# One-core transformer stack: the first norm by channel halves, lambdas later, shift's modulation sums among the first projections, FFN step 0 in other banks, two square roots folded into one

## The reference, cut to what matters

```python
# block 1, two layers l = 0, 1
mod = silu(c) @ ada_w[l] + ada_b[l]        # 1024 -> 6 * 1024
shift1, scale1, gate1, shift2, scale2, gate2 = split(mod, 6)
h = rms_norm(x, norm1_g[l]) * (1 + scale1) + shift1
z = h @ w_in[l]                            # q, k, v, ga, gb, gates
lam = exp(sum(lambda_q1 * lambda_k1)) - exp(sum(lambda_q2 * lambda_k2)) + lambda_init
u = causal_depthwise_conv(ga * sigmoid(gb), 31 taps)
x = x + (1 + gate1) * ((g_attn * y_attn + g_conv * y_conv) @ w_out[l])
h2 = rms_norm(x, norm2_g[l]) * (1 + scale2) + shift2
x = x + (1 + gate2) * ((silu(h2 @ Wg) * (h2 @ Wu)) @ w_ffn_out[l])
# end of block 1, and of block 2: a norm of the stream, and at once the norm of the next block
x = rms_norm(x, final_g); h = rms_norm(x, next_g)
```

## Time and profile before

| what | value |
|---|---|
| median of 3 runs | 2552.34 us (2552.05 to 2553.14) |
| the profiled execution | 2553.99 us, its span 2552.1 us |
| PE busy | 2396.1 us, 94% |
| DVE busy | 1965.9 us, 77% |
| ACT busy | 1442.5 us, 57% |
| PE clock, mean of the span | 0.972 of full |
| read from HBM | 649.32 MB, 255 GB/s |

### The profile page before, as it was taken

How to read it: one execution, slowest core, us unless ns; L and a number is a source line. 1 busy time by engine, 2 the same in 40 slices (tenths; PEclk the granted TensorE clock), 3 DMA queues, 4 the chain that set the end, 5 groups by cost and what they waited for, 6 DMA issues and landing times.

```text
span 2552.1 us, 32705 instructions
## 1 busy us (share of the span) xinstructions
PE 2396.1 (94%) x11965; PEld 2001.3 (78%) x11965; DVE 1965.9 (77%) x1889; ACT 1442.5 (57%) x1418; POOL 17.6 (1%) x33
## 2 busy tenths in 40 slices
PE   4996999998999899799999969999999999999997
PEld 4865788867788798797887968888888888888886
DVE  6888778687687656675445748898989888888897
ACT  2553433546443454464434527777777777777775
POOL 0000000000000000000000000000000000000000
PEclk8997999999999899899999979999999999999998
DMA  8358699534598445455555429999999999999995
GB/s 326 124 173 297 226 317 321 187 121 164 167 329 300 145 163 187 131 170 173 188 183 165 165 83 331 361 340 350 350 340 359 333 366 334 366 334 366 331 368 180
DMA packets 435139, 651.79 MB, mean 255 GB/s; under 512 B 20688, under 2 KB 324432, under 8 KB 435040
## 3 DMA queue, kind: packets, MB, share of 16 engines
q1 hardware_dynamic: 432880, 643.59, 74.0%
q0 software_dynamic: 2160, 6.85, 0.8%
HBM read 649.32 MB, written 1.05 MB: 255 GB/s over the span
## 4 chain that ended last, share of the span: by engine, by line
PE 84%; DVE 9%; ACT 3%; issue 3%; DMA 1%; SPq 0%; DVEq 0%; POOL 0%; ACTq 0%
PE pair L1894 25%; PE pair L1896 25%; PE pair L1895 25%; DVE rest L1079 2%; PE pair L1929 2%; PE tb L2107 2%; DVE aw L1417 1%; ACT head L677 1%; DVE aw L1098 1%; PE pair L2017 1%; PE tb L1972 1%; DMA x<-in_x 1%; ACT aw L706 1%; DVE hT L1200 0%; DVE gat L1825 0%
## 5 line engine op out<-in xcount | busy, mean ns | idle before, releaser
L1079 DVE TENSOR_TENSOR rest<-raw,head 128x2048 fp32r<-128x2048 f32 x546 | 1249.2, 2292 | 296.2 <-ACT head L677 276.4
L677 ACT ACTIVATE head<-raw 128x2048 fp32r<-128x2048 f32 x546 | 1043.2, 1912 | 308.4 <-PE pair L1896 284.9
L1894 PE MATMUL pair<-head,hTh 128*128 128x512 f32 x1864 | 749.4, 402 | 21.2 <-DVE qkv L1509 6.8
L1896 PE MATMUL pair<-head,hTl 128*128 128x512 f32 x1864 | 731.5, 392 | 0.0
L1895 PE MATMUL pair<-rest,hTh 128*128 128x512 f32 x1864 | 730.6, 392 | 0.0
L1894 PEld LDWEIGHTS pair<-head,hTh 128*128 128x128 f32 x1864 | 352.5, 189 | 100.7 <-issue 16.3
L1896 PEld LDWEIGHTS pair<-head,hTl 128*128 128x128 f32 x1864 | 352.0, 189 | 75.0
L1895 PEld LDWEIGHTS pair<-rest,hTh 128*128 128x128 f32 x1864 | 353.0, 189 | 69.3 <-issue 1.5
L1894 PE MATMUL pair<-head,aTh 128*128 128x512 f32 x776 | 307.1, 396 | 2.6 <-issue 2.6
L1895 PE MATMUL pair<-rest,aTh 128*128 128x512 f32 x776 | 303.8, 392 | 0.0
L1896 PE MATMUL pair<-head,aTl 128*128 128x512 f32 x776 | 303.7, 391 | 0.0
(11 more groups left out here) (312 smaller groups left out, 1706.9 us busy)
## 6 DMA issues: line engine op xcount, KB each, us to landing
raw<-in_moe_w_gate SPq DMA_DIRECT2D x224, 512.0 KB, 6.0
raw<-in_moe_w_up SPq DMA_DIRECT2D x224, 512.0 KB, 7.1
raw<-in_moe_w_down SPq DMA_DIRECT2D x224, 512.0 KB, 6.7
raw<-in_w_in SPq DMA_DIRECT2D x152, 512.0 KB, 4.7
raw<-in_ada_w SPq DMA_DIRECT2D x96, 512.0 KB, 5.8
raw<-in_w_ffn_in SPq DMA_DIRECT2D x88, 512.0 KB, 5.5
raw<-in_w_ffn_out SPq DMA_DIRECT2D x44, 512.0 KB, 5.5
raw<-in_w_out SPq DMA_DIRECT2D x40, 512.0 KB, 4.8
```

The source lines that it names most:

```text
L677: act.activation(head[:, c.split, :], raw[:, c.raw, :], ACT.Copy).then_inc(heads_done, 1)
L1079: dve.tensor_tensor(rest[:, c.split, :], raw[:, c.raw, :], head[:, c.split, :].bitcast(F32), ALU.subtract).then_inc(rests_done, 1)
L1894: pe.matmul(out_, lh, rh, start=start, stop=False, skip_group_check=True)
L1896: return pe.matmul(out_, ll, rh, start=False, stop=stop, skip_group_check=True)
```

## The change

In the words of the code before: (a) the first norm is evacuated by channel halves: both tiles' first four channel blocks, then the rest of the first weight chunk, their two `hTl`, then the second halves. PE's first weight chunk needs only the first halves. (b) x is loaded after two modulation chunks instead of after four, and the diagonals are made after five. (c) The lambdas' dot products and rows move behind the rest of gb0's second chunk and around the angles; their spread over the partitions goes on PE between gb0 and q0. (d) Slice (0, 3), shift2, is accumulated (in a row of `xn`) from four chunks that now stand around gb0's second chunk, and summed between q0 and k0. (e) The eight chunks of slices (0, 2) and (0, 4) spread: one each ahead of yattn0.1, yconv0.0 and yconv0.1, two ahead of the first chunk of wout0.0, one each ahead of the next three. The sums of (0, 2) come after wout0.0 on PE instead of before. (f) Step 0 of the three dense FFNs uses the second bank pair, and step 1 need not wait for its product. (g) At the two double norms the second root is taken directly from mean square + 1e-6 times the first one; the first root itself, which the stream needs, comes after the splits.

```diff
         if l == 0:
             queue_mods((0, 0), (0, 1))
             plan_mods(8)
-            queue_mods((0, 2), (0, 3), (0, 4))
+            queue_mods((0, 3), (0, 2), (0, 4))
         plan_norm()
         w = a["w_in"][l]
         plan_linear(f"ga{l}", w, 512, "act", 1536)
-        plan_linear(f"gb{l}", w, 512, "act", 2048)
+        plan.job(f"gb{l}", "act")
+        plan.jobs[f"gb{l}"] = plan.jobs[f"gb{l}"][:2] + (2,) + plan.jobs[f"gb{l}"][3:]
+        for ch, src in enumerate(column_chunks(w, 2048)):
+            plan_mods(2 if l == 0 and ch == 1 else 0)
+            plan.weight(src)
+        plan_mods(2 if l == 0 else 0)
...
+        plan_mods(1 if l == 0 else 0)
         plan_linear(f"yattn{l}.1", a["w_attn_o"][l], NT, "dve", NT, rows=KW)
         plan.split(f"conv{l}")
         for j in range(2):
-            plan_mods(2 if l == 0 else 0)
+            plan_mods(1 if l == 0 else 0)
             plan_linear(f"yconv{l}.{j}", a["w_conv_o"][l], NT, "dve", j * NT, rows=KW)
...
-                plan_mods(2 if l == 0 else 0)
+            for ch, src in enumerate(column_chunks(a["w_out"][l], j * NT)):
+                plan_mods((2 if (j, ch) == (0, 0) else 1) if l == 0 else 0)
...
-            if (k, j) in ((0, 2), (0, 3), (0, 4)):
+            if (k, j) == (0, 3):
+                return xn[:, 1, :]
+            if (k, j) in ((0, 2), (0, 4)):
...
 
             for n, (_, _, parts) in enumerate(plan.seq):
-                if n == 4:
...
-                for t in range(T):
-                    turned_split(0, t)
+                feed(1)
+                for t, half in HALVES_FIRST:
+                    split(f"norm0.{t}{half}", 4 * half, 4 * half + 4, slice(t * P, (t + 1) * P))
...
             def norm_of_ffn(n, k, steps, twice=False):
 
...
+                silu_gate(At(c0 + 1), s0, T, 0, ffn_banks(k)[1:])
...
                     feed(last_chunk("ga0") + 1 + AHEAD)
+                    act.wait_ge(sem("lam_dots"), 1)
+                    act.activation(lam4, lam4, ACT.Exp).then_inc(sem("lam_exp"), 1)
                     sines(0)
...
+                if squared is None:
+                    r = rstd[:, t:t + 1]
+                else:
+                    r, both, q = second_root[:, t:t + 1], rstd_sq[:, t:t + 1], scaled_squares[:, t, 0:1]
+                    dve.wait_ge(sem("first_mean"), tally["mean"])
+                    dve.wait_ge(sem("squared"), squared)
+                    did(dve.tensor_tensor(both, squares[:, t, 1:2], first_mean[:, t:t + 1], ALU.add))
+                    did(dve.tensor_tensor(q, q, scaled_squares[:, t, 1:2], ALU.add))
+                    now()
+                    dve.scalar_tensor_tensor(out=scaled_mean[:, t:t + 1], in0=both, scalar=1e-6, in1=q,
+                                             op0=ALU.mult, op1=ALU.add).then_inc(sem("scaled_mean"), 1)
                 tally["root"] += 1
                 dve.wait_ge(sem("root"), tally["root"])
                 did(dve.reciprocal(r, r))
                 now()
...
+                dve.tensor_scalar(diag[:, t, :], ident, r, None, ALU.mult).then_inc(sem("diag_ready"), 1)
...
+                tally["root"] += 2
+                dve.wait_ge(sem("root"), tally["root"])
+                did(dve.reciprocal(rstd, rstd))
+                now()
...
+                seen[0] = 5
...
+                for half in range(2):
+                    for t in range(T):
+                        evac_turned(0, t, half, scale, shift)
+                    if half == 0:
+                        feed(1)
+                    for t in range(T):
+                        rest_turned(0, t, half)
...
-            for n in range(4):
+            dve.memset(first_mean, 1e-6).then_inc(sem("first_mean"), 1)
+            for n in range(5):
                 mod_chunk(n)
...
                     feed(last_chunk("ga0") + 1 + AHEAD)
+                    lambda_dots()
                     dve.wait_ge(sem("positions_landed"), 16)
                     did(dve.tensor_copy(angle, posi))
                     now()
                     angles(0)
+                    lambda_rows()
                 feed(last_chunk(f"gb{l}") + 1 + AHEAD)
...
+                if l == 0:
+                    dve.wait_ge(sem("lam_spread"), 1)
+                    did(dve.tensor_copy(lamc[:, 0:2], tb[0][:, 0:2]))
...
+                if l == 0:
+                    mod_take(0, 3)
...
+                linear(f"wout{k}.0", NT, splits=(f"mix{k}.0", f"mix{k}.1"))
                 for part in ((0, 2, 0), (0, 2, 1)) if k == 0 else ():
-                    mod_sum(*part)
-                linear(f"wout{k}.0", NT, splits=(f"mix{k}.0", f"mix{k}.1"))
-                for part in ((0, 3),) if k == 0 else ():
                     mod_sum(*part)
...
-                gate_up(At(c0), s0, 0, (1,), 0, s0, banks)
+                gate_up(At(c0), s0, 0, (1,), 0, s0, banks[1:])
                 ready(f"norm{n}.11")
-                gate_up(At(c0 + 1), s0, 1, (1,), 0, None, banks)
...
+                    ffn_step(At(c0 + 2 + 3 * s), s0 + s, (0, 1), s == 0, 0, int(s == 0), banks, FFN_SUMS.get((k, s), ()))
...
                 linear(f"gb{l}", 512, turn=True)
+                if l == 0:
+                    pe.wait_ge(sem("mod_read"), 2)
+                    pe.wait_ge(sem("lam_rows"), 1)
+                    pe.matmul(tb[0][:, 0:2], ones[0:1, :], lam4[:, 0:2], start=True, stop=True).then_inc(sem("lam_spread"), 1)
                 linear(f"q{l}", 512, turn=True)
+                if l == 0:
+                    mod_sum(0, 3)
                 linear(f"k{l}", 512, turn=True)
```

More of the change, by code:

```diff
@@ L34 @@
 FB = 256
+TILES_FIRST = ((0, 0), (0, 1), (1, 0), (1, 1))
+HALVES_FIRST = ((0, 0), (1, 0), (0, 1), (1, 1))
 F1 = 2816
@@ L151, in plan_norm @@
             plan.job(f"norm{n}.{t}", "dve", counted=False)
-            for half in range(2 if splits else 0):
-                plan.split(f"norm{n}.{t}{half}")
+        for t, half in (HALVES_FIRST if n == 0 else TILES_FIRST) if splits else ():
+            plan.split(f"norm{n}.{t}{half}")
     def plan_linear(name, w, cols, evac, n0=0, rows=KD, unsplit=False):
@@ L723, in root @@
                 tally["mean"] += new_mean
-                act.wait_ge(sem("first_mean"), tally["mean"])
-                act.wait_ge(sem("squared"), tally["squared"])
-                act.activation(rstd[:, t:t + 1], squares[:, t, 1:2], ACT.Sqrt, bias=first_mean[:, t:t + 1]).then_inc(sem("root"), 1)
                 if twice:
@@ L730, in root, with first_root, stream_roots @@
                     act.activation(second_root[:, t:t + 1], scaled_mean[:, t:t + 1], ACT.Sqrt).then_inc(sem("root"), 1)
+                    return
+                act.wait_ge(sem("first_mean"), tally["mean"])
+                act.wait_ge(sem("squared"), tally["squared"])
+                first_root(t)
+            def first_root(t):
+                act.activation(rstd[:, t:t + 1], squares[:, t, 1:2], ACT.Sqrt, bias=first_mean[:, t:t + 1]).then_inc(sem("root"), 1)
+            def stream_roots():
+                act.wait_ge(sem("first_mean"), tally["mean"])
+                act.wait_ge(sem("squared"), tally["squared"])
+                for t in range(T):
+                    first_root(t)
             def load_root_table():
@@ L929, in _ @@
             act.activation(cact, pcol("c", 0, 8), ACT.Silu).then_inc(sem("cond_ready"), 1)
-            act.wait_ge(sem("lam_dots"), 1)
-            act.activation(lam4, lam4, ACT.Exp).then_inc(sem("lam_exp"), 1)
             norm_of_input()
@@ L1072, in _ @@
             fed = [0]
-            tally = {"squared": 0, "half": 0, "root": 0, "tile0": 0, "y": 0}
+            tally = {"squared": 0, "half": 0, "root": 0, "tile0": 0, "y": 0, "mean": 1}
             seen = [0]
@@ L1333, in norm_of_input @@
                     mod_take(*part)
-                for t, half in ((0, 0), (0, 1), (1, 0), (1, 1)):
-                    evac_turned(0, t, half, scale, shift)
-                for t, half in ((0, 0), (0, 1), (1, 0), (1, 1)):
-                    rest_turned(0, t, half)
+                for half in range(2):
[3 more added lines that the diff above has]
+                        feed(1)
+                    for t in range(T):
+                        rest_turned(0, t, half)
             def angles(k):
```

75 lines of the change are left out of this document (29 added, 46 removed).

## The result

The changed kernel takes 2529.61 us in the median of 4 runs (2528.53 to 2531.70), the kernel before 2552.56 on the same chip (2552.05 to 2553.14). The ratio is 0.9911, 95% interval 0.9894 to 0.9928. That is 22.95 us less; 17.8 were forecast (2534.5 us), and the range, 2528.5 to 2542.5, holds it. The profiled executions, 2553.99 and 2529.09, lie 24.9 apart, their spans 24.8.

What follows compares the result with a forecast made beforehand. PE was taken as the bound (84% of the chain of waits, DVE 9%), so only its waits and clock count. From 2552.3 us, +4.5 - 14.0 - 6.8 - 1.5 = -17.8 gave 2534.5 us, range 2528.5 to 2542.5.

Steps and rivals of the forecast that it cites:

- The start: Up to k0's end: first projection 6.2 us early, then a 6 us stall at q0; k0 ends 4.5 us later.
- 2 to 4: At q0's first chunk: the 3.0 us lost to half clock could be 2 to 4 in any one run.
- All of the 6.2 is given back: At q0: PE starts its projections 6.2 us early, but stands 6 us and q0 begins at 77.0 to 77.2.
- The mixer's last stage: Layer 0, turn of convolution to turn of norm: 14.0 us gained, 70.4 instead of 84.3; bounds 10 to 17.
- the rest clock and the order of the sums: Mixer's last stage: of 14.0 us gained, 9.4 to 10.7 are four chunks, the remainder clock and sum order.
- FFN step 0: Three dense FFNs: PE's wait for the product ahead of step 1 goes, 3 x 2.27 = 6.8 us; bounds 0 to 7.5.
- Double norms: Two double norms: 0.55 us a tile at three of four tiles, 1.5 us taken; bounds 0 to 2.
- behind it PE has no waits in any of the three FFNs, so it stays: Behind step 0 of the dense FFNs: no later PE wait takes back the 6.8 us gained.
- The stall at q0 doesn't hurt: Rival at q0: the clock stays up, the start costs +1.5 us; 2531.5 us in all, chance 0.12.
- Less from the mixer: Rival: four chunks worth 10 us, second sum or clock at q0 goes badly (+7.5); 2541.5 us, chance 0.16.
- the bank change does nothing: Rival in the FFNs: another wait ends at the same time, so no gain there; 2541.3 us, chance 0.06.
- slower: Rival at the first projections: four chunks bind each one, clock never rises, seven chunks cost +33; 2564.5 us, chance 0.04.

Runs made afterwards that it cites:

- e9: Changed kernel with PE's two sums of the gate's slice put back ahead of wout0.0: 2530.60 us, ratio 0.9916 to the kernel before.
- e3: Kernel before with the faster start alone (first norm by halves, x earlier, lambdas later), slice (0, 3) not moved: 2546.58 us against 2551.95.
- e12: Changed kernel with its faster start undone (first norm, x and lambdas as before); slice, banks and roots kept: 2527.17 us, kernel before 2553.19.
- e6: Kernel before with only PE's two gate sums moved behind wout0.0, all twelve modulation chunks left in place: 2562.26 us against 2551.14.
- e1: Kernel before with only step 0 of the three dense FFNs put on the other banks: 2541.28 us against 2551.95.
- e4: Changed kernel with the last two chunks of slice (0, 3) moved from ahead of q0's first weights to ahead of v0's, their sum behind v0: 2528.11 us.
- e7: e4 with ACT's sines and exponentials behind gb0's copy, DVE's q0 rest ahead of the angles, lambdas' rows and spread later: 2522.00 us.
- e5: Kernel before with only slice (0, 3) moved from the mixer's last stage to the first projections, old start: 2541.89 us against 2551.14.
- e8: The changed kernel measured and profiled again, nothing altered: 2528.70 us against 2551.14 for the kernel before.
- e11: Changed kernel with the load of x back behind the fourth modulation chunk instead of the second: 2528.79 us, kernel before 2552.82.

## Why the prediction held, and where it was short

The forecast missed by 4.9 us (2534.5 against 2529.61), on the safe side. The four terms of the sum came to -18.7 against -17.8, partly since a start that was worse and norms and banks that were better than forecast offset each other; the rest of the miss is clock that the sum didn't have.

- **The start.** Every step came as told: x at 18.17 (18), the modulation's end at 37.0 (36.7), the second sum at full clock 1.95 (1.7), the first projection at 45.67 (45.0), q0 at 77.94 (77.0 to 77.2), a stall of 6.9 (6.0), half clock behind it. k0 and the turn of the convolution are 5.4 late, against 4.5: q0 began 0.9 later than before (77.94 against 77.00) where the forecast had them equal. Two things move that number in other executions of the same program: the loss to half clock at q0's first chunk, 3.0 forecast, was 2.7 here and 1.4 in e9, the second below the "2 to 4" that the prediction allowed, and the turn lies at 181.56, 181.15 and 180.06. "All of the 6.2 is given back" is shown by e3 and e12 together: 5.4 are there without the slice, and nothing with it.
- **The mixer's last stage.** 68.5 us, 70.4 forecast. Of the 15.9, 1.6 are lost between the norm's two tiles, where a stretch of half clock fell (251.2 to 254.6). My split of this term was wrong: "the rest clock and the order of the sums" was 3.3 to 4.6 us, but e9 gives the order 0.1 to 0.9. Four chunks less, with the others spread, are worth 15, more than their DVE time of 2.36 to 2.67 each. That the rest are the waits and the clock that they brought down fits the rows (the wait of 4.5 is gone, that for `merge` is 2.9 less) and is not shown apart. And I missed that the order could not be changed by itself (e6).
- **FFN step 0.** The idle time went at all three places, 2.55 each against the 2.27 of the row.
- **Double norms.** 2.2 against 1.5: the last three tiles gain 0.6 each, as worked out (0.55), and the first, counted at nothing, 0.3.
- **The term that failed** is one that the sum didn't have. I wrote of the FFNs "behind it PE has no waits in any of the three FFNs, so it stays", and took the clock of every later stretch over unchanged. It brought 6.2 us more between the two profiles, about 4 between the medians. The 1.7 at 282 lie where a wait was removed; the others appear and vanish at waits that did not change. By the mean granted clock of the two spans (0.972 and 0.977) the kernel before has some 143 us at half clock, the changed one some 116.
- **The rivals.** "The stall at q0 doesn't hurt" fell in the trace though its 2531.5 is nearer to the measured 2529.61 than the forecast is. "Less from the mixer" fell with 14.3 us gained there, "the bank change does nothing" with e1, and "slower" since PE waited at q0 alone. The time came out below the forecast for a reason that I hadn't priced.

## What to carry to other kernels

Before an engine's work is moved, find its idle time there and count who else spends it: the start and the slice lived on the same 10 us of DVE, were worth 5.4 and 9.3 us alone, and the second to come took the first's away. Read the other engines' lists too (e4 waited for ACT's head behind sines that nobody needed yet; with these and a few more calls moved, e7 is 5 to 6 us below e4 and 6.7 below the changed kernel). And let a feeder that will be late anyway not be met early: here a wait of 1.5 us (e5, e12) cost 1.5, a wait of 6.9 cost the clock as well.

## What the runs showed of the hardware beyond expectation

- The clock came down during a run of 128x1 matmuls while PE's record shows it fully busy: 48 of them took 6.66 us, granted clock 1.00 from 88 to 95 and 0.52 from 95 to 102 us. One kernel was profiled with such a run; that its five executions all lie 6 us or more above the median of the changed kernel fits it. The 16 of the changed kernel at the same place, 1.84 us, left the clock up.
- Two profiles of one kernel (e8) had the same stretches of half clock. But e9 and e11, which have the same program from the first projection to 176 us, had a shorter one at q0 (mean 0.72 from 72 to 84 us in e9, against 0.57). They took q0's first chunk in 7.2 us instead of 8.5 and were 1.3 us ahead behind it. Behind the mixer they lost 1.9 us again in other stretches (2347.6 us from the turn of the convolution to the end, against 2345.7), so that the whole times are nearly the same. The Trainium skill (TensorE: Matmul & The Clock Gate, section "What's actually happening") says that the window which decides on the clock runs free, and that its phase varies from run to run; by these rows the stretches can differ between executions, and by e8 they need not.
- Behind unchanged waits, kernels a few us apart differ by 1 to 6 us in all, and executions of the kernel before by 3.9. Why a given wait brings the clock down in one and not in the other stays open, since no run here moved the phase alone.
